# Three 256-wide matmuls per weight tile in place of one 512-wide and one 256-wide, in a split-float32 transformer trunk

## The reference, cut to what matters

```python
h = h + fox_attention(a_in, fox_w_in[j], ..., fox_w_out[j])        # D x (4 D + 16), D x D
h = h + diff_attention(a_in, diff_w_in[j], ..., diff_w_out[j], ...) # D x 3 D, D x D
h = h + conv_ffn(rms_norm(h, ffn_norm[i]), ffn_w_in[i], ...)       # D x 2 F, then F x D; twice
```

## Time and profile before

| | |
|---|---|
| median of 3 runs | 2557.04 us (2547.58 to 2559.7) |
| the profiled execution's own time | 2557.04 us |
| its span, first to last instruction | 2555.2 us |
| mean granted TensorE clock | 0.973 |
| busy: TensorE / VectorE / ScalarE | 96% / 62% / 47% |
| moved by DMA | 435.21 MB, 170 GB/s |

### The profile page before, as it was taken

How to read it: one execution, slowest core, us unless ns; L and a number is a source line. 1 busy time by engine, 2 the same in 40 slices (tenths; PEclk the granted TensorE clock), 3 DMA queues, 4 the chain that set the end, 5 groups by cost and what they waited for, 6 DMA issues and landing times.

```text
span 2555.2 us, 39956 instructions
## 1 busy us (share of the span) xinstructions
PE 2447.6 (96%) x14179; PEld 2146.7 (84%) x14179; DVE 1585.0 (62%) x1947; ACT 1190.2 (47%) x1590; POOL 11.7 (0%) x21
## 2 busy tenths in 40 slices
PE   4899889999999999999999999979999999999997
PEld 3688768878888888888888999968888888888886
DVE  4566556666666666665555666656666666665553
ACT  3344334444555555554444444434555555554443
POOL 1000000000000000000000000000000000000000
PEclk7899989999999999999999999989999999999998
DMA  5657676745666666655555555536556666655553
GB/s 114 115 152 155 109 125 157 153 138 182 190 188 185 184 197 185 188 182 188 186 188 181 167 183 175 166 112 194 183 182 197 186 189 186 187 180 192 184 184 123
DMA packets 435132, 435.21 MB, mean 170 GB/s; under 512 B 15782, under 2 KB 434063, under 8 KB 434575
## 3 DMA queue, kind: packets, MB, share of 16 engines
q1 hardware_dynamic: 431520, 431.02, 59.0%
q0 software_dynamic: 672, 2.12, 0.3%
q10 hardware_dynamic: 2894, 1.46, 0.2%
HBM read 432.42 MB, written 2.12 MB: 170 GB/s over the span
## 4 chain that ended last, share of the span: by engine, by line
PE 89%; DMA 5%; DVE 3%; ACT 2%; issue 1%; ACTq 0%; DVEq 0%; SPq 0%
PE acc_even L396 27%; PE acc_odd L396 26%; PE acc_even L400 14%; PE acc_odd L400 13%; DMA raw<-in_fox_w_in_dram 5%; PE acc_even L412 1%; PE acc_even L413 1%; PE acc_even L414 1%; DVE w_lo L1000 1%; ACT w_hi L738 1%; PE acc_odd L413 1%; PE acc_odd L412 1%; PE acc_odd L414 1%; PE score_ps L462 0%; PE out_ps L478 0%
## 5 line engine op out<-in xcount | busy, mean ns | idle before, releaser
L1000 DVE TENSOR_TENSOR w_lo<-raw,w_hi 128x1024 fp32r<-128x1024 f32 (+1 forms) x832 | 992.5, 1203 | 814.3 <-ACT w_hi L738 809.2
L738 ACT ACTIVATE w_hi<-raw 128x1024 fp32r<-128x1024 f32 (+1 forms) x832 | 856.5, 1040 | 971.0 <-PE acc_odd L400 415.9
L396 PE MATMUL acc_even<-inputs,w_hi 128*128 128x512 f32 x2176 | 564.7, 402 | 16.9 <-DVE w_lo L1000 14.1
L396 PE MATMUL acc_odd<-inputs,w_hi 128*128 128x512 f32 x1920 | 493.3, 399 | 0.0
L396 PEld LDWEIGHTS acc_even<-inputs,w_hi 128*128 128x128 f32 x2176 | 401.5, 193 | 96.3 <-issue 19.0
L396 PEld LDWEIGHTS acc_odd<-inputs,w_hi 128*128 128x128 f32 x1920 | 349.7, 191 | 67.6 <-issue 3.6
L400 PEld LDWEIGHTS acc_even<-inputs,w_lo 128*128 128x128 f32 x2176 | 300.4, 192 | 22.2
L400 PE MATMUL acc_even<-inputs,w_lo 128*128 128x256 f32 x2176 | 306.1, 284 | 0.0
L400 PEld LDWEIGHTS acc_odd<-inputs,w_lo 128*128 128x128 f32 x1920 | 262.6, 191 | 19.1
L400 PE MATMUL acc_odd<-inputs,w_lo 128*128 128x256 f32 x1920 | 268.1, 283 | 0.0
L396 PE MATMUL acc_odd<-hidden,w_hi 128*128 128x512 f32 x704 | 179.7, 395 | 0.0
(11 more groups left out here) (166 smaller groups left out, 2142.5 us busy)
## 6 DMA issues: line engine op xcount, KB each, us to landing
raw<-in_ffn_w_in_dram SPq DMA_DIRECT2D x352, 512.0 KB, 4.5
raw<-in_fox_w_in_dram SPq DMA_DIRECT2D x128, 512.0 KB, 6.9
raw<-in_ffn_w_out_dram SPq DMA_DIRECT2D x128, 512.0 KB, 3.6
raw<-in_diff_w_in_dram SPq DMA_DIRECT2D x96, 512.0 KB, 3.6
raw<-in_ffn_w_out_dram SPq DMA_DIRECT2D x64, 384.0 KB, 3.6
raw<-in_fox_w_out_dram SPq DMA_DIRECT2D x32, 512.0 KB, 4.2
raw<-in_diff_w_out_dram SPq DMA_DIRECT2D x32, 512.0 KB, 4.1
x_rows<-in_x_dram SPq DMA_DIRECT2D x1, 2048.0 KB, 7.8
```

Source lines behind the costliest of these rows:

```text
L396: pe.matmul(acc[bank][:, m, :], w_hi[:, s, kk, c], x[:, k, :, :], start=(k == 0), stop=False)
L738: act.activation(w_hi[:, s, 0:nk, :], raw[:, s, 0:nk, :], ACT.Copy).then_inc(hi_ready, 1)
L1000: dve.tensor_tensor(w_lo[:, s, 0:nk, :], raw[:, s, 0:nk, :], w_hi[:, s, 0:nk, :].bitcast(F32), ALU.subtract).then_inc(lo_ready, 1)
```

## The change

High and low parts get tiles of their own (`in_hi`, `in_lo`, `heads_hi`, ...), and `unit_features` issues three 256-wide matmuls for each weight tile, all into the same 256 columns. The correction half of the banks is no longer used. With it go ScalarE's copy, VectorE's addition of the copy, VectorE's second addition to the residual, and their three semaphores. The tile `correction` goes; some small tiles are laid out anew.

```diff
-    inputs = sb("inputs", [P, DC, 2, SEQ], F32R)
-    in_hi, in_lo = inputs[:, :, 0, :], inputs[:, :, 1, :]
+    in_hi = sb("in_hi", [P, DC, SEQ], F32R)
+    in_lo = sb("in_lo", [P, DC, SEQ], F32R)
...
-    correction = sb("correction", [P, 2, SEQ])
...
-        def unit_features(const, i, stride, k0, nk, last_k, x, bank):
+        def unit_features(const, i, stride, k0, nk, last_k, x_hi, x_lo, bank):
...
             for m in range(2):
                 for kk in range(nk):
                     k, c = k0 + kk, slice(m * P, (m + 1) * P)
-                    pe.matmul(acc[bank][:, m, :], w_hi[:, s, kk, c], x[:, k, :, :], start=(k == 0), stop=False)
-            for m in range(2):
-                for kk in range(nk):
-                    k, c = k0 + kk, slice(m * P, (m + 1) * P)
-                    mm = pe.matmul(acc[bank][:, m, SEQ:2 * SEQ], w_lo[:, s, kk, c], x[:, k, 0, :],
-                                   start=False, stop=(k == last_k))
+                    o = acc[bank][:, m, 0:SEQ]
+                    pe.matmul(o, w_hi[:, s, kk, c], x_hi[:, k, :], start=(k == 0), stop=False)
+                    pe.matmul(o, w_hi[:, s, kk, c], x_lo[:, k, :], start=False, stop=False)
+                    mm = pe.matmul(o, w_lo[:, s, kk, c], x_hi[:, k, :], start=False, stop=(k == last_k))
             mm.then_inc(multiplied, 1)
...
-        def take_correction(bank, const, i, stride, joined, first):
-
-            act.wait_ge(multiplied, RING + const + i * stride)
-            if not first:
-                act.wait_ge(halves_joined, joined - 1)
-            act.activation(correction[:, :, :], acc[bank][:, :, SEQ:2 * SEQ], ACT.Copy).then_inc(correction_ready, 1)
...
-            dve.tensor_tensor(pair, pair, acc[bank][:, :, 0:SEQ], ALU.add).then_inc(x_main, 1)
-            dve.wait_ge(x_main, PAIRS * (stage - 1) + 1 + b)
-            dve.tensor_tensor(pair, pair, acc[bank][:, :, SEQ:2 * SEQ], ALU.add).then_inc(x_updated, 1)
+                return dve.tensor_tensor(pair, pair, acc[bank][:, :, 0:SEQ], ALU.add)
...
-            dve.wait_ge(correction_ready, joined)
-            dve.tensor_tensor(dst, acc[bank][:, :, 0:SEQ], correction[:, :, :], ALU.add).then_inc(halves_joined, 1)
-            dve.wait_ge(halves_joined, joined)
-            return dve.tensor_tensor(dst, dst, two_wide(rstd), ALU.mult)
+            return dve.tensor_tensor(dst, acc[bank][:, :, 0:SEQ], two_wide(rstd), ALU.mult)
```

More of the change, by code:

```diff
@@ L134, in trunk @@
     rstd = sb("rstd", [P, SEQ])
+    rstd_col = sb("rstd_col", [P, TT])
     square_sum = sb("square_sum", [P, 2, SEQ])
@@ L181, in trunk @@
     top[0] = region
-    hidden = sb("hidden", [P, FC, 2, SEQ], F32R)
-    hidden_hi, hidden_lo = hidden[:, :, 0, :], hidden[:, :, 1, :]
+    hidden_hi = sb("hidden_hi", [P, FC, SEQ], F32R)
+    hidden_lo = sb("hidden_lo", [P, FC, SEQ], F32R)
     g_pad = sb("g_pad", [P, 2, SEQ + 2])
@@ L495, in fox_pair @@
                     pe.wait_ge(drained, B_FOX + 4 * i - 1)
-                unit_features(u + j, i, FOX_UNITS, UK * j, UK, DC - 1, inputs, 0)
+                unit_features(u + j, i, FOX_UNITS, UK * j, UK, DC - 1, in_hi, in_lo, 0)
                 if first and j == 1:
@@ L511, in fox_pair @@
                     pe.wait_ge(drained, B_FOX + 4 * i)
-                unit_features(u + 4 + j, i, FOX_UNITS, UK * j, UK, DC - 1, inputs, 1)
+                unit_features(u + 4 + j, i, FOX_UNITS, UK * j, UK, DC - 1, in_hi, in_lo, 1)
                 if j == 0 and first:
@@ L537, in fox_pair @@
                     pe.wait_ge(drained, B_FOX + 4 * i + 1)
-                unit_features(u + 8 + j, i, FOX_UNITS, UK * j, UK, DC - 1, inputs, 0)
+                unit_features(u + 8 + j, i, FOX_UNITS, UK * j, UK, DC - 1, in_hi, in_lo, 0)
                 if j == 1:
@@ L575, in two_blocks @@
                                 pe.wait_ge(heads_ready, in0 + PAIRS)
-                        unit_features(u + b * UD + j, i, 2 * UD, UK * j, UK, DC - 1, heads, b)
+                        unit_features(u + b * UD + j, i, 2 * UD, UK * j, UK, DC - 1, heads_hi, heads_lo, b)
             two_blocks(0, True)
@@ L668, in diff_head @@
                     pe.wait_ge(in_ready, PAIRS * 2 + 2 * j + 2)
-                unit_features(u + j, i, DIFF_UNITS, UK * j, UK, DC - 1, inputs, 0)
+                unit_features(u + j, i, DIFF_UNITS, UK * j, UK, DC - 1, in_hi, in_lo, 0)
             if first:
@@ L676, in diff_head @@
                     pe.wait_ge(drained, B_DIFF + 3 * i - 1)
-                unit_features(u + 4 + j, i, DIFF_UNITS, UK * j, UK, DC - 1, inputs, 1)
+                unit_features(u + 4 + j, i, DIFF_UNITS, UK * j, UK, DC - 1, in_hi, in_lo, 1)
                 if j == 0 and first:
@@ L1005, in two_wide, with residual_pair @@
             return row[:, None, :].to_broadcast((P, 2, SEQ))
-        def residual_pair(stage, b, g_column, bank):
-            pair = residual[:, bass.ds(2 * b, 2), :]
-            dve.tensor_tensor(pair, pair, acc[bank][:, :, 0:SEQ], ALU.add).then_inc(x_main, 1)
-            dve.wait_ge(x_main, PAIRS * (stage - 1) + 1 + b)
-            dve.tensor_tensor(pair, pair, acc[bank][:, :, SEQ:2 * SEQ], ALU.add).then_inc(x_updated, 1)
+        def residual_pair(stage, b, g_column, update):
+            update(b).then_inc(x_updated, 1)
             finish_pair(stage, b, g_column)
@@ L1030, in finish_pair, with add_block, update @@
             ins.then_inc(in_ready, 1)
+        def add_block(bank):
+            def update(b):
+                pair = residual[:, bass.ds(2 * b, 2), :]
+                return dve.tensor_tensor(pair, pair, acc[bank][:, :, 0:SEQ], ALU.add)
+            return update
         def take_mean(sems, wide, n, epsilon):
@@ L1199, in fox_pair @@
                 if j == 11:
-                    scale_block(gate[:, :, :], 0, J_FOX + 3 * i + 3).then_inc(drained, 1)
+                    scale_block(gate[:, :, :], 0).then_inc(drained, 1)
                     finish_rstd(k_norm_sems, i + 1, head_rstd[:, :, :], 2, k_rstd)
@@ L1237, in two_blocks @@
                     dve.wait_ge(multiplied, RING + u + (b + 1) * UD + i * (2 * UD))
-                    residual_pair(stage, 2 * i + b, g_column, b)
+                    residual_pair(stage, 2 * i + b, g_column, add_block(b))
             two_blocks(0, True)
@@ L1304, in two_blocks @@
                     g_column = V_ATTN + DC * (layer + 1) if layer < DEPTH - 1 else None
-                    residual_pair(stage + 1, 2 * i + b, g_column, b)
+                    residual_pair(stage + 1, 2 * i + b, g_column, add_block(b))
             two_blocks(0, False)
```

48 lines of the change are left out of this document (14 added, 34 removed).

## The result

The changed kernel took 2630.31 us (median of 4 runs, 2629.8 to 2631.43) against 2554.32 us: ratio 1.0288, 95% interval 1.0264 to 1.0314. The forecast was 2599 us with a range up to 2618: the direction was right, the size was not (+76 us where +42 was forecast).

The account below looks back on a forecast made before the run. TensorE's matmul pace was taken to bound the kernel almost everywhere. 43.4 + 3.5 + 0.7 - 3.8 - 1.8 = +42.0 us on 2557.04 gave 2599 us, 1.6% slower, with a range from 2568 to 2618.

Parts of the forecast that it names:

- TensorE sets the time almost everywhere; its pace is read from starts.: Whole kernel: TensorE busy 2447.6 of 2555.2 us, so time is the number of matmuls times their pace; only forgetting heads have gaps.
- 120.0 ns on the inputs, 117.5 on hidden.: Price per 256-wide matmul after the change: +43.4 us over 4096 triples on inputs, +3.5 us over 1408 on hidden.
- Rows 6: Trace rows of tokens-first units on the inputs tiles: 96 matmuls at 120.0 ns each, taken as the price on inputs.
- Rows 7: Trace rows of 48 forget-logit matmuls at 118.3 ns each; as price on inputs the milder rival, 2578 us, chance 0.17.
- Why `inputs` is slower in short matmuls than `hidden`: Left unexplained: 256-wide matmuls run slower on inputs, pairs do not; after the change nothing wide takes the loss back.
- The removed joins, -3.8 us.: Copies and additions dropped, nearly all hidden under TensorE: -3.8 us on the path, ends 0 and 18, capped near 10.
- The loading of weights in the heads, -1.8 us.: Forgetting heads: 28 of 128 units wait for HBM, hiding that share of 8.2 us of dearer matmuls, -1.8 us.
- The new layout: High and low tiles, 2 KB less in front of heads and hidden: costed at nothing, any effect left to the ends.
- Code as a rival.: Down-projection loop body grows from 704 to 1056 loads and matmuls, fetched anew each turn: +56 us, 2655 us, chance 0.04.

Follow-up runs that it names:

- experiment 2: Kernel before and changed kernel, both with the forgetting heads' weights loaded from another matrix with rows of 24576 bytes in place of 32832: 2499.55 and 2541.21 us.
- split_only: Kernel before with three 256-wide matmuls per weight tile, but accumulator halves and all joins kept: 2631.35 us, ratio 1.0296.
- Experiment 3: Kernel before with TensorE's down-projection loops written out, code from 29 to 40 packets: 2588.28 us; also with 35 packets 2579.93, with 56 packets 2542.83.
- after_shift64: Changed kernel with raw, w_hi, w_lo and all tiles behind them moved up by 64 bytes: 2559.32 us, ratio 1.0025 to the kernel before.
- after_64_both: Changed kernel with 64 bytes added ahead of the weight ring and 32 ahead of heads and hidden: 2532.08 us, ratio 0.9890 to the kernel before.

## Why the prediction was wrong

- *TensorE sets the time almost everywhere; its pace is read from starts.* Right.
- *120.0 ns on the inputs, 117.5 on hidden.* Right: 119.9 and 117.1 measured. The 10.6 ns for each triple on the inputs made most of the 41.4 us behind the heads (38.8 forecast; with the joins kept it was 39.4, and in experiment 2 it was 36.3). Rows 6 were the right price. Rows 7 were the wrong one; their stationary tile lies at another distance (32, not 0). On `heads` a matmul took 118.7 ns in place of 117.5, some 2 us in all.
- *Why `inputs` is slower in short matmuls than `hidden`, "the trace does not say".* The experiments say that it is where the tiles lie: shifted by 64 bytes, the same matmuls on the inputs take 113.3 ns in gate and up. That nothing wide is left to take the loss back was the right reading; that the loss could be had back by the placing of a tile was not seen. Why the place matters stays open.
- *The removed joins, -3.8 us.* Mis-sized. Behind the heads nothing shows: split_only, which keeps them, has 2055.7 us against 2057.75. In the heads without valleys the changed kernel ends 1.3 us earlier, although the dearer pace would add 8.2 us there. An estimate of the relief in the heads is so some 9 us, where 3.1 was forecast (if no wait hides the pace).
- *The loading of weights in the heads, -1.8 us.* **This is the step that failed.** I spread 28 waits for HBM evenly over 128 units, as cover for dearer matmuls, and took the speed of loading as given. The waits lie in valleys of 16 units each. The change moved the valleys from pairs 0 and 4 to pairs 1 and 5, where both are paid in full: +36.7 us in the heads where +3 was forecast. Experiment 3 shows +33.8 us by code alone, and experiment 2 shows nothing left of it without the valleys. The page before had the valleys in its row of GB/s; I did not read it by slices, and the DMA share of 0.67 in the earlier trace rows is a mean over them.
- *The new layout "I cost at nothing".* It did not fail: without valleys nothing is left for it to explain. It is not "2 KB less" in front of `heads` and `hidden` but 1920 bytes, since the small tiles grew by 128; the distance from hidden to the ring went from 224 to 96, and the pace stayed (117.5 and 117.1).
- *Code as a rival.* It was put as a refetch of loops; there was none (TensorE is busy 150 of 150 us in a window over turns of the down loop). The factors in brackets there give 352, the matmuls alone; with their loads they are the 704. The code does matter, but by another way, which the prediction put at nothing: with its size the valleys move.
- The Trainium skill's page DMA: Bandwidth & Descriptors (section "Latency and other measured facts") reports that a row pitch in HBM near a large power of two costs bandwidth, that a pad of 4 KB heals it and one of 192 bytes does not. The rows here have a pitch of 32 KB and 64 bytes, a smaller one than it names. Rows of 24576 bytes had no valleys (experiment 2), which would agree, but they lay in another matrix, so pitch and place are not told apart. Which columns are hit, and why the program's size decides it, no run here shows: where the matrix lies in HBM is only my inference.

## What to carry to other kernels

Before pricing an edit, look at the traffic by slices: a stage that is fed too slowly in places will pay for an edit by where those places fall, and an edit that only changes the size of the program can move them. Compare two variants once with the disturbed source of data replaced, as in experiment 2, to separate what the edit costs from what it moved. When matmuls of one shape run at different paces on different tiles, shift one tile by 32 or 64 bytes before concluding that the shape is dear: here 64 bytes were worth about 70 us (after_shift64 against the changed kernel), and with the second shift about 100 us (after_64_both). Read the pace in more than one stage: at one distance it took two values.

## What the runs showed of the hardware

- The pace of a float32r matmul of 256 columns with a weight load each lies between 113.3 and 120 ns and changes when a tile is moved in SBUF. By the distance between the tile that streams and the one that is loaded it is 119.9 at 0, 118.2 at 32, about 117.1 to 118.7 at 96, and 113.4 or 117.8 at 64. The Trainium skill (TensorE: Matmul & The Clock Gate, section "Step-by-step: what each phase is for") says that loading the next weights takes no SBUF read bandwidth from the running matmul; a pace that goes by the distance of the two tiles does not fit that, though it could have another cause.
- A pair of 512 and 256 columns feels it less: 348.9 ns at distance 0 and 346.0 at 64 (on the inputs, 400 us over 2293 and 2312 matmuls), where the triple goes from 359.8 to 339.8.
- Loading [128 x 4 x 256] tiles from rows of 32832 bytes runs at 85 to 97 GB/s in two of eight column blocks, four blocks apart, and at about 154 elsewhere (in the kernel with 56 packets of code at 120 to 134). The DMA engines are busy throughout those blocks in the changed kernel (1.01), but not in the kernel before (0.64 and 0.66). From another matrix, with rows of 24576 bytes, there is no such block. This costs the kernel before some 58 us (experiment 2).
- Which two blocks are slow changed with the size of TensorE's code: pairs 0 and 4 with 29 packets, pairs 1 and 5 with 35 to 56.
